# Experts of a hybrid diffusion step: four buffers for gathered rows in place of two, slot lists made in other memory, other waits for weights

## The chip, the cores and the metric

One core of a Trainium2 chip runs the whole step as one program. The metric is device time in microseconds (us) of that core; the median of three runs is compared.

## The reference

Two trunk layers work on 640 tokens (512 latent, 128 context) of width 1024 in float32. Layer 0 has HGRN2 heads beside latent attention, layer 1 gated convolution channels beside a convolution module. Each layer ends with a hierarchical mixture of experts, and only this part is touched here:

```python
p_group = softmax(t @ w_group); g_sel = argmax(p_group); p_g = max(p_group)
e_in = expert logits inside the chosen group; top_v, top_i = top_k(e_in, 2)
w_top = softmax(top_v) * p_g
hid = silu(t @ w_gate[e]) * (t @ w_up[e])      # 32 experts, FF = 128
out = sum over the two chosen e of w_top * (hid @ w_down[e])
x = layer_norm(ALPHA * x + gate * out)         # R5 holds the rows of this gate
```

## The kernel before

One program per engine, written by hand; semaphores set the order. A layer comes in this order: projections and mixer, output projection with normalisation and router, experts, combination.

*Router and lists.* VectorE works out the choice of each token and then the lists of rows of each slot (lines 1753 to 1820). A slot block has SL = 64 rows of one expert. Two blocks make a pair, so the 32 experts are NP0 = 16 main pairs (numbered 0 to 15). Experts with more than 64 rows spill into extra blocks, which are done in rounds ("quads") of two extra pairs. This data has one round in layer 0 (extra pairs 16 and 17 below) and two in layer 1 (16 to 19). HOT, PAIR, SLOT and other work areas of the lists lie in the tile mix_cm (OTF, lines 456 to 460). The lists end up in TIY, and rows_ready tells of them: first the gather rows, then the scatter rows.

*Weights.* SyncE loads three matrices of 128 x 1024 float32 words (0.52 MB) for each expert, six loads per pair (load_expert, line 643). There are four weight slots, pair u using slot u % 4; the words of slot 3 lie in scratch and in mix_cm, on top of the list areas (EXPERT_AT, line 574). So in front of pair 3 SyncE waits for rows_ready (line 710), and for pair u it waits until pair u - 4 is done (at_least(sp, m["down"], u - 3), line 711). Extra pairs use slots 0 and 1 and wait for down at 15 and 16, that is for main pairs 14 and 15, at line 723, and in the second round for the extra pair two before.

*Rows.* GpSimd gathers the rows of a pair from h_rows in memory into XG, two buffers (line 827), and scatters the results from ZT, two buffers, into expert_rows (line 833). In its loop (lines 848 to 865) it waits for the turn of pair u, issues the gather of u + 2, waits for the results of u in ZT (ya, yv), and issues the scatter of u. At pairs 6, 8 and 10 it has some other work (residual rows, two loads of normalisation rows).

*Computation of a pair.* TensorE turns the gathered rows (turn, line 2461, 8 transposes), multiplies by gate and up (gate_up, line 2473, 32 products), turns the hidden values (2480) and multiplies by down (2490, 8 products). In the order of its program: gate_up(u), turn(u + 1), turn_hidden(u), down(u). ScalarE and VectorE copy halves of the turned rows and of the results.

*R5.* The gate rows of the combination, 128 x 2048 words in scratch words 4096 to 6143, are loaded by SyncE before the output projection of their layer (lines 688 and 695) and used at line 1900. G1, the gate rows of the first residual, lies in GR; it is last used at line 1730, before the lists are made.

*Combination.* When all scatters are done (moe_done, line 889) SyncE loads expert_rows back, TensorE sums them with their weights (line 2005), and the second normalisation follows.

Of the kernel before, what the change touches and what calls it, by code (L numbers as in the profile page):

```python
# [17 lines left out]
KD = D // 128  # L18
NT = 5
NLAT = 512  # L20
NTOK = 640
# [19 lines left out]
NCOL = NPAIR + 2  # L41
# [169 lines left out]
def build(nc, A, O):  # L211
# [7 lines left out]
    with ctx:  # L219
# [101 lines left out]
        def moe_sems(l):  # L321
            names = ["w0", "w1", "w2", "w3", "wd0", "wd1", "wd2", "wd3", "xw0", "xw1", "xwd0", "xwd1", "g0", "g1", "t", "xa", "xv", "gu", "sg", "hid", "ht", "hc",
                     "down", "ya", "yv", "s0", "s1", "s_ix", "pool_passed"]
            return {n: sem(f"moe{l}_{n}") for n in names}
        MS = [moe_sems(l) for l in range(2)]


# [125 lines left out]
        XG = z(10240, 2048).rearrange("p (b d) -> p b d", b=2)  # L453
        XGT = z(12288, 2048).rearrange("p (b d) -> p b d", b=2)
        GG, GT = z(15040, 160), z(15200, 160)
        HOT = OTF[:, 512:1792].rearrange("p (i s) -> p i s", i=2 * NT)
        PAIR = OTF[:, 2100:2100 + 2 * NT * NCOL].rearrange("p (i c) -> p i c", i=2 * NT)
        SLOT, SLOTM, PNUM, INPAIR, BASE = [OTF[:, 2980 + 10 * i:2990 + 10 * i] for i in range(5)]
        ROWI, NONE = OTF[:, 3040:3040 + NCOL], OTF[:, 3080:3080 + NCOL]
        KROW = OTF[:, 3120:3120 + NCOL]  # L460
# [131 lines left out]
        def _(sp):  # L592
# [50 lines left out]
            def load_expert(l, e, p, i, first, second):  # L643
                m = MS[l]
# [8 lines left out]
                sp.dma_start(expert_gu(p, i)[:, 0:1024], g).then_inc(m[f"{first}{p}"], 16)  # L653
                sp.dma_start(expert_gu(p, i)[:, 1024:2048], u).then_inc(m[f"{first}{p}"], 16)
                sp.dma_start(expert_down(p, i), dn).then_inc(m[f"{second}{p}"], 16)

            for l in range(2):
# [29 lines left out]
                if l == 0:  # L687
                    load_rows(0, 5, R5, d_g1)
                else:
# [5 lines left out]
                    load_rows(1, 5, R5, d_g1)  # L695
# [8 lines left out]
                for u in range(NP0):  # L704
# [4 lines left out]
                    if u == 3:  # L709
                        sp.wait_ge(rows_ready, 2 * l + 2)  # L710
                    at_least(sp, m["down"], u - 3)
                    for i in range(2):
                        load_expert(l, 2 * u + i, u % 4, i, "w", "wd")
# [3 lines left out]
                with sp.If(quads > 0):  # L717
                    with sp.Fori(0, quads) as j:
                        for u in range(4):
                            e = sp.value_load(EXI[0:1, bass.ds(j * 4 + u, 1)], min_val=0, max_val=NE - 1)  # L720
                            if u % 2 == 0:

                                sp.wait_ge(m["down"], j * 2 + (NP0 - 1 + u // 2))
                            load_expert(l, e, u // 2, u % 2, "xw", "xwd")
# [14 lines left out]
        def _(pool):  # L739
# [53 lines left out]
            for l in range(2):  # L793
# [32 lines left out]
                def gather(par, rows):  # L826
                    nc.gpsimd.indirect_dma_start(  # L827
                        out=XG[:, par, :], out_offset=None, in_=HD[:, :],
# [1717 lines left out]
```

## Time and profile before

| | us |
|---|---|
| median of three runs | 1415.01 (1414.82 to 1421.27) |
| the profiled execution | 1423.75 |
| its span, first to last instruction | 1421.9 |
| TensorE busy | 1197.5 (84%) |
| VectorE busy | 574.1 (40%) |
| ScalarE busy | 344.5 (24%) |
| GpSimd busy | 188.9 (13%) |
| moved by DMA | 266.59 MB, mean 187 GB/s |
| chain that ended last: TensorE 69%, DMA 16%, VectorE 7% | |

The busy share is an average over stages with different limits. The expert stage of layer 0 lies at about 640 to 830 us, that of layer 1 at about 1175 to 1381 us. Of the chain, 10% are gathers (scratch<-h_rows), 2% loads of w_up. In the rows below, L2461 is line 2461, PE is TensorE, SPq the queue of SyncE, and a window's DMA share is the mean busy share of the 16 DMA engines.

### The profile page before, as it was taken

The numbers are of one execution on the slowest core, as the hardware profiler recorded it, in microseconds if no ns is written. First come the engines' busy times: TensorE is split into PE (matmuls) and PEld (weight loads), VectorE is DVE, ScalarE is ACT, GpSimd is POOL, SyncE is SP. The second block draws the span as 40 slices with busy tenths as digits, with TensorE's granted clock in tenths as the row PEclk, the third lists the DMA queues.
The fourth block names the chain that finished last, engine by engine and source line by source line (L and its number), as shares of the span: only waits on it lengthen the run. The fifth ranks groups of instructions, "written<-read, shape, count | busy, mean of one in ns | idle before, by whom it ended". The sixth has DMA issues, their size and how long they took to land.

```text
span 1421.9 us, 17080 instructions
## 1 busy us (share of the span) xinstructions
PE 1197.5 (84%) x6597; PEld 696.4 (49%) x6597; DVE 574.1 (40%) x1123; ACT 344.5 (24%) x687; POOL 188.9 (13%) x175
## 2 busy tenths in 40 slices
PE   4999999999999989966877767999979966877755
PEld 2554455555465764544544434555544544544432
DVE  2123332200456665552311133199946552311217
ACT  1334444311145441111111115110132111111112
POOL 1000000000000010301332115200000301242120
PEclk9999999999999999976988988999998977989987
DMA  9423566833101061075999763211102065999764
GB/s 342 164 98 132 192 229 240 311 109 139 47 19 67 9 249 60 30 274 188 409 409 388 274 245 119 94 59 60 60 0 104 30 262 201 403 410 402 260 236 176
DMA packets 98369, 266.59 MB, mean 187 GB/s; under 512 B 12572, under 2 KB 14883, under 8 KB 97139
## 3 DMA queue, kind: packets, MB, share of 16 engines
q1 hardware_dynamic: 82176, 230.36, 43.0%
q0 software_dynamic: 15792, 35.04, 6.6%
q8 instruction: 53, 0.87, 0.2%
q14 instruction: 26, 0.21, 0.0%
q10 hardware_dynamic: 322, 0.12, 0.0%
HBM read 257.65 MB, written 28.79 MB: 201 GB/s over the span
## 4 chain that ended last, share of the span: by engine, by line
PE 69%; DMA 16%; DVE 7%; issue 3%; ACT 3%; SPq 1%; ACTq 0%; POOL 0%; POOLq 0%; DVEq 0%
PE ps L2034 17%; PE ps L2045 15%; DMA scratch<-h_rows,gather_scatter_rows 10%; PE ps L2473 5%; PE ps L2490 4%; PE ps L1953 3%; PE ps L2170 3%; PE ps L2461 2%; DMA weights<-in_moe_w_up 2%; PE ps L2332 2%; PE ps L2313 2%; PE ps L2137 1%; PE ps L2005 1%; PE ps L2057 1%; PE ps L2187 1%
## 5 line engine op out<-in xcount | busy, mean ns | idle before, releaser
L2034 PE MATMUL ps<-h_cm,weights 128*128 128x512 f32 (+1 forms) x896 | 247.2, 438 | 1.1 <-ACT h_cm L961 1.1
L2034 PEld LDWEIGHTS ps<-h_cm,weights 128*128 128x128 f32 x896 | 137.0, 192 | 115.1 <-issue 114.8
L2045 PE MATMUL ps<-weights,mix_cm 128*128 128x512 f32 x288 | 127.3, 600 | 1.0 <-ACT mix_cm L1147 1.0
L2473 PE MATMUL ps<-weights,scratch 128*64 128x256 f32 x704 | 90.5, 414 | 14.9 <-DMA weights<-in_moe_w_up 13.0
L1612 DVE SCALAR_TENSOR_TENSOR scratch<-scratch,taps_cm 128x655 f32<-128x655 f32 x120 | 101.5, 897 | 2.5 <-ACT scratch L1196 1.0
L2461 PE MATMUL ps<-consts,scratch 128*128 128x128 f32 x304 | 50.3, 316 | 60.5 <-DMA scratch<-h_rows,gather_scatter_rows 60.5
L2045 PEld LDWEIGHTS ps<-weights,mix_cm 128*128 128x128 f32 x288 | 54.7, 192 | 67.0 <-issue 66.9
L2473 PEld LDWEIGHTS ps<-weights,scratch 128*64 128x64 f32 x704 | 62.8, 151 | 47.8 <-issue 34.9
L2045 PE MATMUL ps<-weights,h_cm 128*128 128x512 f32 (+1 forms) x240 | 83.3, 506 | 2.8 <-DMA weights<-in_ab_w_in 2.8
L2461 PEld LDWEIGHTS ps<-consts,scratch 128*128 128x128 f32 x304 | 41.4, 199 | 76.8 <-DMA scratch<-h_rows,gather_scatter_rows 48.2
L1857 DVE TENSOR_TENSOR scratch<-ps,scratch 128x128 f32<-128x128 f32 x38 | 11.1, 291 | 131.2 <-ACT scratch L1236 131.1
L2045 PEld LDWEIGHTS ps<-weights,h_cm 128*128 128x128 f32 x240 | 42.4, 194 | 43.5 <-issue 40.4
L833 POOL DMA_INDIRECT expert_rows<-scratch,gather_scatter_rows x32 | 33.1, 1034 | 196.6 <-ACT scratch L1242 140.8
L1544 DVE SCALAR_TENSOR_TENSOR mix_cm<-mix_cm,gate_rows,ps 128x128 f32<-128x128 f32 x152 | 46.0, 345 | 28.7 <-PE ps L2278 26.6
L1867 DVE COPY scratch<-ps 128x512 f32<-128x512 f32 x38 | 26.3, 691 | 69.9 <-PE ps L2490 69.9
L1289 DVE COPY mod_parts<-ps 128x512 f32<-128x512 f32 x24 | 16.6, 691 | 93.6 <-PE ps L1953 93.6
L2490 PE MATMUL ps<-weights,scratch 128*64 128x512 f32 x176 | 45.3, 635 | 9.6 <-issue 6.4
L1228 ACT ACTIVATE scratch<-ps 128x512 f32<-128x512 f32 x38 | 22.7, 597 | 120.2 <-PE ps L2461 120.2
L827 POOL DMA_INDIRECT scratch<-h_rows,gather_scatter_rows x36 | 37.0, 1026 | 69.8 <-DVE router_small L1820 44.6
L1242 ACT ACTIVATE scratch<-ps 128x512 f32<-128x512 f32 x38 | 22.7, 597 | 88.9 <-PE ps L2490 88.9
L819 POOL DMA_DIRECT2D h_rows<-scratch x10 | 5.7, 574 | 280.0 <-DVE scratch L1693 280.0
L1236 ACT ACTIVATE scratch<-ps 128x128 f32<-128x128 f32 x38 | 10.6, 278 | 131.7 <-PE ps L2473 131.7
(405 smaller groups left out, 1875.7 us busy)
## 6 DMA issues: line engine op xcount, KB each, us to landing
weights<-in_mod_w SPq DMA_DIRECT2D x13, 2048.0 KB, 8.8
weights<-in_moe_w_gate SPq DMA_DIRECT2D x44, 512.0 KB, 9.1
weights<-in_moe_w_up SPq DMA_DIRECT2D x44, 512.0 KB, 10.8
weights<-in_moe_w_down SPq DMA_DIRECT2D x44, 512.0 KB, 11.6
x_tm<-in_mod_w SPq DMA_DIRECT2D x10, 2048.0 KB, 8.7
weights<-in_ab_w_in SPq DMA_DIRECT2D x6, 2048.0 KB, 12.0
weights<-in_cd_w_in SPq DMA_DIRECT2D x5, 2048.0 KB, 15.9
h_cm<-in_moe_w_gate SPq DMA_DIRECT2D x16, 512.0 KB, 11.1
```

Source lines behind the costliest of these rows:

```text
L827: nc.gpsimd.indirect_dma_start(out=XG[:, par, :], out_offset=None, in_=HD[:, :], in_offset=bass.IndirectOffsetOnAxis(ap=rows, axis=0), bou ...
L833: nc.gpsimd.indirect_dma_start(out=YD[:, :], out_offset=bass.IndirectOffsetOnAxis(ap=rows, axis=0), in_=ZT[:, par, :], in_offset=None, bou ...
L1544: ins = V.scalar_tensor_tensor(out=nxt, in0=state_before(i, n, step, hh), scalar=HE[:, u % 2, at:at + 1], in1=bank(4 + j)[:, hh * 128:hh * ...
L1612: ins = V.scalar_tensor_tensor(out=CO[:, j, 0:655], in0=UP[:, j, k:k + 655], scalar=CW[:, 4 * k + j:4 * k + j + 1], in1=CO[:, j, 0:655], o ...
L1953: ins = T.matmul(ps("mod", l, c)[32 * j:32 * j + 32, 0:512], CT[:, k, :], w[:, k, :], start=(k < 4), stop=(k >= 4))
L2034: ins = T.matmul(ps(*name)[:, a:b], w[:, k, col:col + 128], HT[:, k, a:b], start=(k == 0), stop=(k == KD - 1))
L2045: ins = T.matmul(ps(*name)[:, at:at + w.shape[2]], src[:, k, t * 128:t * 128 + 128], w[:, k, :], start=(k == 0), stop=(k == KD - 1))
L2170: ins = T.matmul(ps("s", 2 * p + i, t)[:, a:b], q[rows, tc], k[rows, ka:ka + b - a], start=(rope == 0), stop=(rope == 1))
L2313: ins = T.matmul(bank(3), w[:, k, j * 128:j * 128 + 128], HT[:, k, 0:512], start=(k == 0), stop=(k == KD - 1))
L2461: ins = T.transpose(turned_bank(k // 4)[:, (k % 4) * 128:(k % 4) * 128 + 128], rows[:, k, :], ident)
L2473: ins = T.matmul(pair_bank(u)[SL * i:SL * i + SL, 0:256].rearrange("p (g f) -> p g f", g=2), XGT[:, u % 2, at:at + SL], w[:, k, :, :], sta ...
L2490: ins = T.matmul(result_bank(u, b)[SL * i:SL * i + SL, :], HIDT[:, u % 2, SL * i:SL * i + SL], w[:, b * 512:b * 512 + 512], start=True, st ...
```

## The change

- XG becomes four buffers. The two new ones lie in scratch words 4096 to 6143, the words of R5. The gather of pair u + 4 is issued at the turn of pair u; four gathers are issued at the start. Buffers 2 and 3 have semaphores of their own (gathered), shared by both layers.
- The areas of the slot lists (HOT, PAIR, SLOT and so on) move from mix_cm to GR, the tile of G1. The wait for rows_ready in front of pair 3's weights goes.
- The extra pairs' weights wait for x_slot, which GpSimd raises after the results of main pairs 12 and 13, and in the rounds after those of each extra pair.
- R5 is no longer loaded by SyncE before the output projection, but by GpSimd at pair 15, after its turn; VectorE waits for it (d_r5) where it used to wait for d_g1.
- The weights' semaphores are shared by both layers (pair_gu, pair_down), with values counted on, and TensorE's loop is written out for main and extra pairs. Its order of work is the same.

The core of the diff, without renamings that go with it:

```diff
-        XG = z(10240, 2048).rearrange("p (b d) -> p b d", b=2)
+        XG = [z(10240, 1024), z(11264, 1024), z(4096, 1024), z(5120, 1024)]
-        HOT = OTF[:, 512:1792].rearrange("p (i s) -> p i s", i=2 * NT)
-        PAIR = OTF[:, 2100:2100 + 2 * NT * NCOL].rearrange("p (i c) -> p i c", i=2 * NT)
-        SLOT, SLOTM, PNUM, INPAIR, BASE = [OTF[:, 2980 + 10 * i:2990 + 10 * i] for i in range(5)]
+        HOT = GR[:, 0:1280].rearrange("p (i s) -> p i s", i=2 * NT)
+        PAIR = GR[:, 1280:1280 + 2 * NT * NCOL].rearrange("p (i c) -> p i c", i=2 * NT)
+        SLOT, SLOTM, PNUM, INPAIR, BASE = [GR[:, 1600 + 10 * i:1610 + 10 * i] for i in range(5)]
@@ SyncE
-                if l == 0:
-                    load_rows(0, 5, R5, d_g1)
-                else:
+                if l == 1:
                     retire(LAST_IN_SLOT1[1])
...
                     load_rows(1, 3, R3, d_r)
-                    load_rows(1, 5, R5, d_g1)
...
-                    if u == 3:
-                        sp.wait_ge(rows_ready, 2 * l + 2)
                     at_least(sp, m["down"], u - 3)
                     for i in range(2):
-                        load_expert(l, 2 * u + i, u % 4, i, "w", "wd")
+                        load_expert(l, 2 * u + i, u % 4, i, pair_gu[u % 4], pair_down[u % 4])
...
-                                sp.wait_ge(m["down"], j * 2 + (NP0 - 1 + u // 2))
-                            load_expert(l, e, u // 2, u % 2, "xw", "xwd")
+                                sp.wait_ge(m["x_slot"], j * 2 + (1 + u // 2))
+                            load_expert(l, e, u // 2, u % 2, m[f"xw{u // 2}"], m[f"xwd{u // 2}"])
@@ GpSimd
-                for u in range(2):
+                for u in range(4):
                     gather(u, TIY[:, 0, u:u + 1])
...
                     pool.wait_ge(m["t"], u + 1)
-                    pool.wait_ge(m[f"g{par}"], 16 * (u // 2 + 1))
-                    gather(par, TIY[:, 0, u + 2:u + 3])
+                    pool.wait_ge(g_sems[u % 4], (64 * l if u % 4 > 1 else 0) + 16 * (u // 4 + 1))
+                    if u < NP0 - 2:
+                        gather(u % 4, TIY[:, 0, u + 4:u + 5])
+                    elif u == NP0 - 1:
+
+                        pool.wait_ge(d_mod, MOD_DMAS * 2)
+                        pool.dma_start(R5, MODD[l, 3].partition_broadcast(128)).then_inc(d_r5, 16)
 
                     pool.wait_ge(m["ya"], u + 1)
                     pool.wait_ge(m["yv"], u + 1)
+                    if u in (NP0 - 4, NP0 - 3):
+
+                        pool.sem_inc(m["x_slot"], 1)
                     at_least(pool, m[f"s{par}"], 16 * (u // 2))
                     scatter(par, TIY[:, 1, u:u + 1])
...
                             pool.wait_ge(m["ya"], j * 2 + (NP0 + u + 1))
                             pool.wait_ge(m["yv"], j * 2 + (NP0 + u + 1))
+                            pool.sem_inc(m["x_slot"], 1)
@@ VectorE
-                dve.wait_ge(d_g1, 32 if l == 0 else 48)
+                dve.wait_ge(d_g1, 16 * (l + 1))
...
-                dve.wait_ge(d_g1, 32 * (l + 1))
+                dve.wait_ge(d_r5, 16 * (l + 1))
@@ TensorE
-                    pe.wait_ge(m[f"g{u % 2}"], g0 + 16 * (u // 2 + 1))
+                    pe.wait_ge(landed, value)
```

## Rows read from the trace of the kernel before

**Rows 1.** Who TensorE waits for, 640 to 835 us: us in total, times, longest.
```profile
PE ps L2461 <- DMA scratch<-h_rows,gather_scatter_rows: 30.5, 8, 9.5
...
PE ps L2473 <- DMA weights<-in_moe_w_up: 5.1, 2, 4.4
```

**Rows 2.** Stretches: us; PE, PEld, DVE, ACT, POOL busy; clock, DMA share, GB/s.
```profile
660.00:664.00 4.00, 4.00 (x29) 2.62 (x26) 0.29 (x1) 0.28 (x1) 0.00 (x0) 0.78 0.02 5
667.00:784.00 117.00, 90.97 (x620) 57.70 (x616) 28.65 (x72) 18.47 (x38) 37.52 (x32) 0.90 1.01 394
680.00:700.00 20.00, 17.73 (x133) 11.52 (x133) 9.11 (x27) 4.14 (x8) 5.32 (x5) 1.00 1.03 408
784.00:803.00 19.00, 16.81 (x107) 9.85 (x107) 4.03 (x9) 2.94 (x6) 4.01 (x4) 0.91 0.52 177
1200.00:1317.00 117.00, 90.92 (x631) 57.87 (x627) 28.75 (x72) 18.64 (x39) 37.52 (x32) 0.91 1.00 395
1317.00:1333.00 16.00, 14.04 (x98) 8.41 (x98) 4.03 (x9) 2.85 (x6) 4.01 (x4) 1.00 0.57 188
```

**Rows 3.** Timeline of TensorE: start us, us, line, shapes, [idle before <- releaser].
```profile
657.56 5.72 PE L2473 MATMUL ps<-weights,scratch 128*64 128x256 f32 x32 [0.88 <-DVE scratch L1849]
...
663.21 1.16 PE L2461 MATMUL ps<-consts,scratch 128*128 128x128 f32 x8
...
670.28 1.16 PE L2461 MATMUL ps<-consts,scratch 128*128 128x128 f32 x8
...
719.85 1.97 PE L2461 MATMUL ps<-consts,scratch 128*128 128x128 f32 x8 [3.25 <-DMA scratch<-h_rows,gather_scatter_rows]
...
784.21 1.71 PE L2461 MATMUL ps<-consts,scratch 128*128 128x128 f32 x8 [2.68 <-DMA scratch<-h_rows,gather_scatter_rows]
...
808.53 5.33 PE L2473 MATMUL ps<-weights,scratch 128*64 128x256 f32 x32 [4.37 <-DMA weights<-in_moe_w_up]
...
818.18 3.67 PE L2473 MATMUL ps<-weights,scratch 128*64 128x256 f32 x32 [0.75 <-DMA weights<-in_moe_w_up]
...
823.30 1.94 PE L2490 MATMUL ps<-weights,scratch 128*64 128x512 f32 x8 [0.43 <-DVE scratch L1861]
...
1360.19 5.36 PE L2473 MATMUL ps<-weights,scratch 128*64 128x256 f32 x32 [3.51 <-DMA weights<-in_moe_w_up]
...
1369.24 3.67 PE L2473 MATMUL ps<-weights,scratch 128*64 128x256 f32 x32
```

**Rows 4.** Timeline of SyncE: issues of expert weights, start us and us.
```profile
646.34 0.33 SPq L653 DMA_DIRECT2D scratch<-in_moe_w_gate  x1
...
666.93 0.33 SPq L653 DMA_DIRECT2D weights<-in_moe_w_gate  x1
...
796.41 0.36 SPq L653 DMA_DIRECT2D weights<-in_moe_w_gate  x1
...
1348.92 0.35 SPq L653 DMA_DIRECT2D weights<-in_moe_w_gate  x1
```

**Rows 5.** Chain that ended last: start us, us, what.
```profile
646.99 7.62 DMA scratch<-h_rows,gather_scatter_rows
...
767.33 3.68 PE ps L2490 x8
...
1068.98 16.84 PE ps L2057 x32
```

**Rows 6.** The gather, line 827: time to landing of all 42.
```profile
DMA to landing us min/median/max: 2.1/8.1/13.2
```

**Rows 7.** Timeline of VectorE at the output projection of layer 1.
```profile
1079.72 2.29 DVE L1720 TENSOR_TENSOR scratch<-scratch,ln_rows 128x2048 f32<-128x2048 f32 x1 [8.68 <-DMA scratch<-mod_rows]
...
1086.58 1.22 DVE L1730 TENSOR_TENSOR scratch<-ps,gate_rows 128x1024 f32<-128x1024 f32 x1
```

**Rows 8.** What the DMA engines moved from 664 to 818 us.
```profile
DMA packets 16998, 55.13 MB, mean 358 GB/s; under 512 B 3566, under 2 KB 3566, under 8 KB 16987
...
q1 hardware_dynamic: 12091, 44.03, 73.4%
```

## What the change is expected to do

> **What bounds the kernel now.** I read four views in this order: who TensorE waits for in the expert stage of layer 0, the stretches of both expert stages, what the DMA engines carried, and then the single instructions.
>
> The first view says that TensorE waits 30.5 us in 8 long pieces for gathered rows and only 5.1 us for expert weights, both of these in the extra pairs [rows 1]. Taken alone, this asks for more gather buffers. The second view corrects it. From the first release of a weight slot to about the landing of the last main weights, 667 to 784 us, the DMA engines are busy at 1.01 and carry 394 GB/s, and in layer 1 they do the same from 1200 to 1317 us [rows 2]. So in those 117 us the gather is late because it shares engines that are already full. Twelve pairs of weights come in there, 117 / 12 = 9.75 us per pair. TensorE alone needs 7.07 us per pair at full clock (two successive turns, 663.21 and 670.28) [rows 3]. The bound is DMA bandwidth, and the gather wait is where it shows.
>
> Behind this stretch the engines fall to 0.52 for 19 us (177 GB/s); in layer 1 it is 0.57 for 16 us [rows 2]. The reason is in the issues: the first extra weights leave at 796.41 us, when pair 14 is done [rows 4], though their slot was last used by pair 12. TensorE meanwhile works off pairs 13 to 15 with nothing coming in behind them. There is another hole before the first release: the engines are at 0.02 from 660 to 664 us [rows 2], since all four slots are full.
>
> **The change part by part.** I count in bytes and in the time at which the last extra weights can be used, because everything behind that (last pair, scatter, reading back, combining) is untouched.
>
> *Slot lists in other memory, no wait before the fourth pair.* Today the weights of pair 3 leave at 646.34 us [rows 4], beside the first gather, which takes 7.62 us on the chain [rows 5]; gathers go down to 2.1 us and have a median of 8.1 us [rows 6]. Pair 3 will leave right behind pair 2, near 632 us, and its 3.15 MB (two experts, three matrices of 0.52 MB) take 8 us at 394 GB/s; queued behind pairs 0 to 2 they are in by about 648 us. The first gather should then land at 5 to 6 us, so the first release comes at about 664.5 instead of 666.93 us [rows 4]: 2.4 us earlier (bounds 0 and 3.5). In layer 1 the loads start later against the router, and I take 1.5 us. The vector instructions that make the lists are the same ones; only their addresses differ, and I cost that at nothing.
>
> *Four gather buffers.* A gather for pair u+4 is issued at the turn of pair u, so each has some 28 us for what takes 8.1 us, at most 13.2 us [rows 6]. The 30.5 us wait goes. What is late next is the weights: TensorE catches up with them after some eight pairs and then waits 9.4 - 7.07 = about 2.3 us in each pair. This part alone gives little at the rate of the stream. It gives TensorE's position: at the end of the stream it is at most one pair behind the weights, where today it has three or four pairs to do. It also moves two gathers, 0.6 MB, into the empty stretch before the first release.
>
> *Extra weights after pairs 12 and 13 (x_slot).* Today their release waits for pairs 14 and 15. Now they follow pair 15's weights with hardly a pause, so the hole at 784 to 803 us closes. x_slot is raised by GpSimd, in line with its gathers and scatters; behind the results of pair 12 this is some 1 us later than TensorE's own signal, while two to three pairs of weights are queued at the DMA engines. The second round in layer 1 has only these two slots and keeps its dependence on the first extra pair; there I charge the 1 us.
>
> *R5 moved to the end of the main pairs.* 128 x 2048 x 4 bytes = 1.05 MB go into the full stream: +2.6 us at 408 GB/s, hidden behind nothing in layer 0, since the last weights are behind it. The load is on GpSimd's queue, ahead of the scatter of pair 15 and of the extra pairs; the scatter's buffer is wanted two pairs, some 18 us, later, and R5 itself only in the combination. Its removal from the beginning of a layer frees nothing on the path: in layer 1 VectorE does wait 8.68 us for such rows [rows 7], but the first result of the output projection is ready at 1085.82 us [rows 5] and VectorE, through with its row operations, takes it up at 1086.58 [rows 7]; I take 0 (bounds 0 and 1 us). The added wait on d_mod there has been satisfied for long.
>
> *Sum for layer 0.* From 664 to 818 us 55.13 MB were moved, 44.03 MB of them on the queue of the weights, which is 14 pairs [rows 8]. Of the new order the same stretch holds + 1.05 (R5) - 0.6 (two gathers), about 55.6 MB. At 394 GB/s that is 141 us, at 408 GB/s (the rate inside the full stretch, 680 to 700 us, without its ramp at the start [rows 2]) 136 us. With the release at 664.5 the last extra weights are in at 800.8 to 805.6 us; I take 803. Today the last extra pair's products begin at 818.18 us [rows 3]. Gain 15 us (bounds 12.5 and 17.5).
>
> *Sum for layer 1.* The first two extra pairs come 15 us earlier as well: weights at about 1327 and 1336 us. The first of them ends at 1334, its slot is refilled from 1335, and from issue to use that took 1360.19 - 1348.92 = 11.3 us [rows 3, 4]: 1346.3. The last pair's slot is free at 1343.4 + 1; with the same 11.3 us its products begin at 1355.7 us, against 1369.24 now [rows 3]: gain 13.5 us (bounds 9 and 17).
>
> *Clock.* After a wait TensorE may begin at its low level: 4.37 us of idle cost the 32 products 5.33 instead of 3.67 us, 3.25 us gave a turn of 1.97 us, 2.68 us one of 1.71 instead of 1.16 us [rows 3]. My 2.3 us waits lie just below these. I charge 0.75 us for the last pair of each layer, 1.5 us.
>
> Total 15 + 13.5 - 1.5 = 27 us. The span 1421.9 becomes 1394.9, and the profiled execution's time of 1423.75 becomes 1396.8. The three runs of the kernel before had 1415.01 as their median, 8.7 us under that execution. Subtracting the same 27 us gives 1388.
>
> One rule of the Trainium skill speaks against this: "DMA: Bandwidth & Descriptors", section Specifications, gives about 358 GB/s as what memory yields to one core. By it 55.6 MB would need 155 us and layer 0 would gain nothing (819.8 against 818.18). The trace disagrees: 394 GB/s stand for 117 us in both layers [rows 2].
>
> **The rivals.**
> *The early loads work, the deeper gathers don't help.* GpSimd works in order, so each gather still stands behind the results and the scatter before it; if gathers slow as the weight queue deepens, TensorE keeps today's pace and only the hole is filled. Extra weights are then in before TensorE gets to them: 4 us of waiting and 1.7 us of low clock in front of the first extra pair [rows 3] and about 1 us before the second go, 6.7 us per layer, some 14 in all: 1401. Against: at the worst seen, 13.2 us [rows 6], a gather four pairs ahead is still in time. Chance 0.15.
> *More than forecast.* The stream holds 408 GB/s, no wait costs clock, the second round of layer 1 is as dense as the first: 17.5 + 17, 1380. Chance 0.12.
> *It doesn't do what it says.* A second wait of the same length (the shared semaphores, a GpSimd order that holds x_slot back until pair 15, or the memory rate of the page) leaves the last extra weights where they are: 1411 to 1419. Chance 0.07.
> *Slower, through the clock.* Every pair now has a wait for weights. If it suffices to drop the clock each time, a pair costs 7.07 + 0.81 (turn 1.97 for 1.16) + 2.05 (products 5.72 for 3.67) + 1.74 (second products 3.68 for 1.94) = 11.7 us [rows 3, 5]. Fourteen pairs from 686 us then end at 850, where today the end is 825.2 [rows 3]; with layer 1 that is +50 us, 1465. It decides from a mean pair of (825.2 - 686) / 14 = 9.94 us, that is when over 62% of the pairs run low. Against it: a pair at the low level outlasts the 9.4 us in which weights arrive, so its wait vanishes and TensorE, busy without a break, gets its clock back, as within the products of 657.56 [rows 3]. The skill has it too ("TensorE: Matmul & The Clock Gate", section HAM oscillation): a wait for DMA in every tile can throttle each tile anew; the stretch 667 to 784, with its longer waits, ran at 0.90 [rows 2]. Chance 0.04.
>
> **How the numbers follow.** The forecast has the remaining 0.62; its own range is 1382 to 1397 (gains of 33 and 18 us, near the bounds of the two sums). The range of 8 in 10 takes in the better case, with up to 3 us more should both starts gain their full 3.5 us, and just the partial one: 1377 to 1402. A measurement of this kernel can tell 0.5%, 7 us, from no change. Faster by more, under 1408: 0.62 + 0.15 + 0.12 = 0.89. Within 0.5%: 0.07. Slower by more: 0.04.
>
> **What would show it.** Right: TensorE's wait for gathered rows nearly gone and in its place some ten waits of 2 to 3 us for weights per layer; the DMA engines at 1.0 from about 665 to 800 us without the hole; first extra weights issued near 776 us instead of 796.41; the fourth pair's near 632; the last extra pair's products at about 803 and 1355 us; R5 landed before the combination. Wrong: a hole that stays, gathers over 20 us, a mean pair of 9.75 us although the gathers are in, the low clock in most pairs, or a combination that waits for R5.

## The result and the profile after

The changed kernel takes 1404.85 us (median of 10 runs, 1401.88 to 1408.92). The kernel before, run in the same sessions, takes 1420.51 us (median of 10, 1407.82 to 1424.74). The ratio is 0.990 with a 95% interval of 0.988 to 0.993: the kernel became 1.0% faster, about 14 us. The prediction had the direction right, forecast 27 us and 1388 us, and its range ended at 1402. Of the 16.9 us by which 1388 was missed, 5.5 us are the starting point (the three runs I counted from had a median of 1415.0, ten have 1420.5); the larger part is the gain itself.

| | before | after |
|---|---|---|
| profiled execution, span | 1421.9 us | 1402.6 us |
| expert stage, layer 0 | 178.25 us | 172.65 us |
| expert stage, layer 1 | 195.21 us | 186.62 us |
| weights of pair 3 issued | 646.34 us | 625.62 us |
| first weight slot free, after the first gather's issue | 19.9 us | 16.8 us |
| first extra weights issued | 796.41 us | 771.60 us |
| last extra pair's products begin, layer 0 | 818.18 us | 804.40 us |
| last extra pair's products begin, layer 1 | 1369.24 us | 1348.88 us |

"Expert stage" is from the issue of the first gather to the end of the last extra pair's second products. I use it because the two profiled executions do not start it at the same time: the first gather of layer 0 leaves at 646.99 us before [rows 5] and at 641.78 us after. Those 5.2 us are not the change's: of two experiments below, e5, which is the kernel before with one constant altered, issues it at 642.49 us in its profile, and e4, which has the change, at 647.76 us. At least in part they come from stretches in which the older execution had a low clock (the same 32 records of products near 535 us took 15.57 us there and 13.97 us here). The spans differ by 19.3 us: 5.2 so, 5.6 in the stage of layer 0, 8.6 in that of layer 1, and nothing left over. The stages give 14.2 us, as does the ratio of the runs (1.0%); the two medians lie 15.7 us apart.

Who TensorE waits for after the change, 630 to 830 us (us in total, times, longest); the rows answer to [rows 1]:

```profile
PE ps L2014 <- DMA scratch<-expert_rows: 10.3, 1, 10.3
PE ps L2482 <- DMA weights<-in_moe_w_up: 7.6, 3, 3.4
PE ps L2470 <- DMA scratch<-h_rows,gather_scatter_rows: 6.3, 1, 6.3
PE ps L2482 <- DMA h_cm<-in_moe_w_up: 6.3, 2, 3.5
...
PE ps L2482 <- DMA mix_cm<-in_moe_w_up: 5.7, 2, 3.2
```

Of the 30.5 us in 8 waits for gathered rows one wait is left, that for the first gather, with nothing of the stage ahead of it to hide behind: 6.3 us, 9.5 before. The 21 us of the others are gone. In their place stand 7 waits for expert weights, 19.6 us in all, where the kernel before had 2 with 5.1 us. `weights`, `h_cm` and `mix_cm` are the memories of different slots, so these three rows are one cause. That is the picture the prediction drew. The first row is the read-back behind the stage, which nobody touched.

The next view is what explains the miss: stretches of the kernel after (us; PE, PEld, DVE, ACT, POOL busy; granted clock, DMA share, GB/s), answering to [rows 2].

```profile
658.00:784.00 126.00, 103.52 (x688) 61.18 (x686) 31.51 (x78) 20.61 (x42) 38.45 (x33) 0.92 1.01 397
784.00:792.00 8.00, 6.88 (x49) 4.02 (x46) 1.71 (x4) 1.31 (x3) 1.57 (x2) 1.00 1.03 414
792.00:796.00 4.00, 2.83 (x27) 1.97 (x26) 0.95 (x2) 0.76 (x2) 1.83 (x3) 1.00 0.86 350
796.00:800.00 4.00, 3.57 (x28) 2.19 (x26) 1.18 (x3) 0.88 (x2) 0.39 (x1) 1.00 0.41 161
800.00:804.00 4.00, 1.03 (x6) 0.15 (x2) 0.69 (x1) 0.60 (x1) 0.86 (x2) 0.95 0.24 96
804.00:808.00 4.00, 3.60 (x18) 2.37 (x20) 0.00 (x0) 0.00 (x0) 1.57 (x3) 0.50 0.13 41
```

The engines are full from 658 to 792 us without the hole of 0.52 that [rows 2] had behind 784 us. But they do not stop together. The share falls over 12 us, 0.86, 0.41, 0.24, 0.13: a few engines are still at work while most have nothing to do. And TensorE waits for just those. The chain that ended last has this in it (start us, us, what):

```profile
641.78 4.45 DMA scratch<-h_rows,gather_scatter_rows
...
783.35 20.82 DMA weights<-in_moe_w_up
...
804.40 6.65 PE ps L2482 x32
```

This load, the second w_up of the last extra pair and the fifth of its six loads, takes 20.82 us from its issue, and the products start only when its last piece is in. TensorE's timeline shows that the wait then costs a second time:

```profile
775.75 5.36 PE L2482 MATMUL ps<-h_cm,scratch 128*64 128x256 f32 x32 [2.77 <-DMA h_cm<-in_moe_w_up]
...
793.79 3.67 PE L2482 MATMUL ps<-weights,scratch 128*64 128x256 f32 x32 [1.17 <-DVE scratch L1858]
...
804.40 6.64 PE L2482 MATMUL ps<-weights,scratch 128*64 128x256 f32 x32 [3.37 <-DMA weights<-in_moe_w_up]
...
812.49 1.94 PE L2499 MATMUL ps<-weights,scratch 128*64 128x512 f32 x8 [0.43 <-DVE scratch L1870]
...
1340.05 5.07 PE L2482 MATMUL ps<-weights,scratch 128*64 128x256 f32 x32 [3.58 <-DMA weights<-in_moe_w_up]
...
1348.88 3.67 PE L2482 MATMUL ps<-weights,scratch 128*64 128x256 f32 x32 [0.20 <-DMA weights<-in_moe_w_up]
```

The "32 products" of this document are 32 records: the code has 16 gate and up products for a pair (8 steps for each of two experts), and the trace records each twice. The 32 records take 3.67 us at 2.4 GHz. Behind waits of 2.77, 3.37 and 3.58 us they take 5.36, 6.64 and 5.07 us, at the low level (1.2 GHz) for more than half of it; the stretch 804 to 808 us has a granted clock of 0.50.

### The profile page after: what moved, and what is told of

Read it like the earlier page. It is cut to its first block, busy times and chain, and to the rows that moved or that the text cites. A ratio compares the mean times of both kernels' runs of the same rounds, so it can differ in the third digit from the quotient of the medians.

```text
span 1402.6 us, 17080 instructions
## 1 busy us (share of the span) xinstructions
PE 1194.3 (85%) x6597; PEld 685.8 (49%) x6597; DVE 574.2 (41%) x1123; ACT 344.5 (25%) x687; POOL 190.0 (14%) x177
## 4 chain that ended last, share of the span: by engine, by line
PE 65%; SPq 13%; DMA 8%; DVE 7%; ACT 3%; issue 3%; ACTq 0%; POOLq 0%; DVEq 0%; POOL 0%
PE ps L2043 18%; PE ps L2054 15%; PE ps L2482 4%; SPq L658 4%; SPq L656 4%; SPq L657 4%; DMA weights<-in_moe_w_up 3%; PE ps L1962 3%; PE ps L2179 3%; PE ps L2341 2%; PE ps L2499 2%; PE ps L2322 1%; PE ps L2146 1%; PE ps L2014 1%; PE ps L2470 1%
## 5 line engine op out<-in xcount | busy, mean ns | idle before, releaser
L2482 PE MATMUL ps<-weights,scratch 128*64 128x256 f32 x704 | 96.2, 434 | 26.3 <-DMA weights<-in_moe_w_up 23.3
L2470 PE MATMUL ps<-consts,scratch 128*128 128x128 f32 x304 | 45.7, 295 | 13.2 <-DMA scratch<-h_rows,gather_scatter_rows 13.2
L1245 ACT ACTIVATE scratch<-ps 128x128 f32<-128x128 f32 x38 | 10.6, 278 | 181.7 <-PE ps L2482 181.7
L2470 PEld LDWEIGHTS ps<-consts,scratch 128*128 128x128 f32 x304 | 38.1, 195 | 28.5 <-issue 28.5
L2482 PE MATMUL ps<-scratch 128*64 128x256 f32 x128 | 35.4, 440 | 8.9 <-DMA mix_cm<-in_moe_w_up 8.9
L2482 PE MATMUL ps<-h_cm,scratch 128*64 128x256 f32 x256 | 34.4, 428 | 8.9 <-DMA h_cm<-in_moe_w_up 8.8
```

What stands on the lines that cost most here:

```text
L2470: ins = T.transpose(turned_bank(k // 4)[:, (k % 4) * 128:(k % 4) * 128 + 128], rows[:, k, :], ident)
L2482: ins = T.matmul(pair_bank(u)[SL * i:SL * i + SL, 0:256].rearrange("p (g f) -> p g f", g=2), XGT[:, u % 2, at:at + SL], w[:, k, :, :], sta ...
```

## The experiments

**Theory and rivals.** The mean share had done what the byte count said: from the full stretch to the tail, nothing was missing. So the theory (A) was: the rows of gathers and scatters are spread unevenly over the 16 engines. Each expert has 64 places in a pair's 128, and its tokens fill them from the first partition upward; places without a token are skipped. If an engine serves fixed partitions, those with low ones carry more rows on top of an equal share of the weights, and the last load lands when the fullest engine is through. The rivals were that the deeper gathers or the early extra weights did not do what they should, that R5's 1.05 MB were the burden, and that the deeper queue itself lets the engines drift apart.

All medians stand beside that of the kernel before on the same chip, and "under it" is the distance between the two; "stages" is the sum of the two expert stages in the one profiled execution (before 373.5, after 359.3), good to some us.

| kernel | median us (n) | before | under it | ratio, 95% | stages |
|---|---|---|---|---|---|
| the changed kernel | 1404.85 (10) | 1420.51 | 15.7 | 0.988 to 0.993 | 359.3 |
| e1_spread | 1395.47 (6) | 1417.55 | 22.1 | 0.982 to 0.989 | 348.0 |
| e2_gather_two_ahead | 1413.44 (10) | 1417.55 | 4.1 | 0.994 to 0.998 | 361.0 |
| e3_extras_late | 1408.00 (9) | 1417.55 | 9.5 | 0.992 to 0.996 | 364.0 |
| e4_r5_behind | 1402.24 (4) | 1417.55 | 15.3 | 0.984 to 0.993 | 351.2 |
| e5_before_spread | 1413.59 (10) | 1418.13 | 4.5 | 0.995 to 1.001 | 364.1 |
| e6_spread_r5 | 1393.55 (6) | 1418.13 | 24.6 | 0.981 to 0.987 | 343.7 |
| e7_eights | 1413.06 (10) | 1418.13 | 5.1 | 0.996 to 1.001 | 363.8 |
| e8_spread_r5_order | 1389.59 (6) | 1418.13 | 28.5 | 0.978 to 0.985 | 341.6 |
| e9_order_and_busy | 1389.10 (6) | 1418.97 | 29.9 | 0.974 to 0.982 | 339.2 |
| e10_three_pairs | 1418.05 (10) | 1418.97 | 0.9 | 0.996 to 1.001 | 368.4 |

The changed kernel was not run again beside these ten, and the kernel before stood 1.5 to 3 us higher in its sessions than in theirs. So a difference to 1404.85 us has that much in doubt beside the noise; where it matters, both the distance of the medians and that of the column "under it" are given.

**e1_spread: the same tokens in other partitions.** Only a constant changes, the place that each rank of an expert gets. Eight successive ranks now fall into eight different groups of four partitions.

```diff
-    put("iota_h", slice(None), p[None, :] - (SL - 0.5))
+    r = np.arange(SL)
+    place = 8 * (r % 8) + (r // 8 + 4 * (r % 8 >= 4)) % 8
+    rank = np.argsort(place)
+    put("iota_h", slice(None), (SL * (p // SL) + rank[p % SL])[None, :] - (SL - 0.5))
```

> The changed kernel with one constant altered: the 64 places of a block are taken in an order that goes round the partition groups, so that the about 40 rows which a block holds on average lie evenly over all groups of partitions, in place of the first 40. Nothing is left out. In the changed kernel the last extra weights of layer 0 land at 804 us although the mean DMA share falls to 0.43 at 796 us: a few of the 16 engines are behind. Theory A (the rows of gathers and scatters lie unevenly, and the engines that serve the first places get up to twice the rows): the tail with few engines vanishes, the last extra weights are used 5 to 8 us earlier after the first gather in each layer, 1393 us (1388 to 1397). Theory B (the engines drift apart for another reason, such as unequal speed or the depth of the queue): the tail stays, within 3 us of the changed kernel's 1405.

Measured: 1395.47 us, 9.4 us under the changed kernel (6.4 us by the distances to the kernel before), with the same 17080 instructions and, to 0.01 MB, the same bytes. The tail of the stream of e1 in layer 0 (stretches, columns as above) and, from TensorE's timeline, the last pair's products:

```profile
792.00:796.00 4.00, 4.00 (x30) 2.34 (x26) 0.00 (x0) 0.00 (x0) 0.00 (x0) 0.74 1.02 404
796.00:800.00 4.00, 3.36 (x20) 1.61 (x17) 1.26 (x4) 0.96 (x3) 0.00 (x0) 1.00 0.58 234
800.00:804.00 4.00, 3.67 (x32) 2.65 (x32) 0.61 (x1) 0.54 (x2) 1.39 (x3) 1.00 0.09 32
```

```profile
800.26 3.67 PE L2485 MATMUL ps<-weights,scratch 128*64 128x256 f32 x32 [0.47 <-DMA weights<-in_moe_w_up]
```

The share stays at 1.02 until 796 us and is at 0.09 from 800 us on, where it was 0.24 and 0.13 before the edit. The engines end together. The last pair's wait shrinks from 3.37 to 0.47 us, its products run in 3.67 us. The stages are 165.03 and 183.01 us; the prediction's own sums, 15 - 0.75 and 13.5 - 0.75 us off the stages before, were 164.0 and 182.5. So the sum was right, to about 1 us, for engines that share evenly, and theory A has its mechanism. Its size was smaller than expected: against the first gather the last pair's products begin 4.7 us earlier than in the changed kernel in layer 0 (157.97 for 162.62) and 3.6 us in layer 1, not 5 to 8; the other 3.0 us are the clock of the last pair in layer 0, which I had not counted. Nor is it the tail alone: the first extra weights leave 124.4 us after the first gather, 129.8 in the changed kernel, which fits late engines that hold up the pairs inside the full stretch too.

**e7_eights: which partitions belong together.** The same idea with another step: successive ranks eight partitions apart and nothing else.

```diff
-    rank = np.argsort(8 * (r % 8) + (r // 8 + 4 * (r % 8 >= 4)) % 8)
+    rank = np.argsort(8 * (r % 8) + r // 8)
```

> As e1, but rank r of a block goes to place 8 * (r % 8) + r / 8: for each run of eight neighbouring partitions the same number of rows, but only the first four partitions of each eight are taken up to rank 31. If an engine serves eight neighbouring partitions, this is as even as e1: 1395. If it serves groups of four partitions that alternate (partitions 4n to 4n + 3), then every second group gets up to twice the rows and the time is that of the changed kernel, 1405, or up to 5 us more.

Measured: 1413.06 us, 8.2 us slower than the changed kernel (10.6 by the distances) and so somewhat beyond what I expected. Against e6, run beside it, it is 19.5 us slower, of which e6's other edit, R5 moved, may account for 2 to 3 us. The stretches of e7:

```profile
792.00:796.00 4.00, 2.98 (x16) 1.46 (x16) 1.38 (x2) 1.20 (x2) 0.57 (x1) 1.00 1.00 413
796.00:800.00 4.00, 1.57 (x8) 1.02 (x10) 0.00 (x0) 0.00 (x0) 1.66 (x3) 0.76 0.69 274
800.00:804.00 4.00, 4.00 (x30) 2.38 (x28) 0.06 (x1) 0.28 (x1) 0.00 (x0) 0.82 0.51 201
804.00:808.00 4.00, 3.17 (x20) 1.52 (x20) 1.81 (x4) 1.20 (x2) 0.00 (x0) 1.00 0.36 146
```

Here about half the engines are still busy (0.51) where in e1 almost none is. In this order the first 32 ranks of an expert lie in partitions whose number divided by eight leaves 0 to 3: every other group of four. That they load half the engines, while e1's order loads all, says that partitions 0 to 3 of each eight and partitions 4 to 7 are served by different engines. Four neighbouring partitions as the unit fit this; a smaller unit was not ruled out by a run. The Trainium skill has this ("DMA: Bandwidth & Descriptors", section The descriptor swizzle), for full transfers to 128 partitions: an engine writes four partitions and the four that lie 32 further on, engines 0 to 7 the lower half and 8 to 15 the upper. By that rule e7 puts an expert's first 32 rows on four of its eight engines, and e1 spreads each eight rows over all eight; 1413 and 1395 us agree with it, for gathers and scatters that skip rows too. The trace names no engine by number, so which one is late is not shown. In the stages e7 lies 4.5 us above the changed kernel, less than in the medians.

**e5_before_spread: e1's edit on the kernel before.**

> The kernel before with the one altered constant of e1 (rows of a block spread evenly over the partition groups). Theory A (uneven rows make a few DMA engines late) holds for this kernel as well, but here TensorE works off three pairs behind the last main weights, and a late engine is hidden there; gathers may land a little earlier in the full stretch. Expected 1414 (1409 to 1418) beside a kernel before at 1417. If the even rows are worth the same 10 us here as on the changed kernel, the unevenness limited the full stretch itself, not only what is last to land.

Measured: 1413.59 against 1418.13 us, ratio 0.998 with an interval of 0.995 to 1.001: no more than 7 us and not to be told from nothing. The stage sum is 9.4 us shorter in its one profile, more than the medians bear out. I had expected the unevenness to cost little in the kernel before, because a late engine there has three pairs of work and a hole of 19 us to catch up in. The medians allow that and don't show it: up to 7 us in the interval stand beside 6 to 9 us for the same edit on the changed kernel. The trace speaks against a full cover. Against the first gather, e5 issues its first extra weights 6.0 us earlier than the kernel before (143.4 for 149.4), and this gain arises ahead of the hole. That the change made the unevenness dearer is therefore argued and not shown; shown is that even rows are worth having in the changed kernel.

**e2_gather_two_ahead: two gathers in flight, everything else as changed.**

```diff
-                for u in range(4):
+                for u in range(2):
                     gather(u, TIY[:, 0, u:u + 1])
...
-                    if u < NP0 - 2:
-                        gather(u % 4, TIY[:, 0, u + 4:u + 5])
-                    elif u == NP0 - 1:
+                    gather((u + 2) % 4, TIY[:, 0, u + 2:u + 3])
+                    if u == NP0 - 1:
```

> The changed kernel, but only two gathers are issued at the start and the gather of pair u + 2 is issued at the turn of pair u, as before the change; extra weights, lists and R5 stay as changed. If the deeper gathers carry the gain, TensorE waits some 30 us for gathered rows in each layer again and the time goes back by 7 us or more, to 1412 or above, since only the hole behind the main weights is filled. If the early extra weights carry it (the rival of the prediction), it stays at 1405 within 3 us.

Measured: 1413.44 us, 8.6 us slower than with four (11.6 by the distances). Waits of TensorE in e2, whole span:

```profile
PE ps L2469 <- DMA scratch<-h_rows,gather_scatter_rows: 53.6, 16, 7.0
```

The waits for gathered rows are back, 16 of them in the two layers. So the deeper gathers carry more than half of the whole gain, and the rival of 1401 us ("the deeper gathers don't help") falls by its mechanism, though its number came nearest. The profiled execution of e2 is the fastest of its ten, 5 us below the median; its stage sum is not to be set against the medians.

**e3_extras_late: the first extra weights wait for pairs 14 and 15 again.**

```diff
-                                sp.wait_ge(m["x_slot"], j * 2 + (1 + u // 2))
+                                sp.wait_ge(m["down"], j * 2 + (NP0 - 1 + u // 2))
```

> The changed kernel, but the extra pairs' weights wait for main pairs 14 and 15 again in place of x_slot; four gather buffers stay. Theory: a pair of extra weights needs about 11 us from issue to use; with the wait back, the hole of about 15 us in the DMA engines comes back, and the time is 1412 to 1420. If the deeper gathers alone carried the gain it would stay at 1405 within 3 us.

Measured: 1408.00 us, only 3.2 us slower than the changed kernel (6.1 by the distances); I had expected 1412 to 1420. Stretches of e3 and, from SyncE's timeline, its first issue of extra weights:

```profile
776.00:780.00 4.00, 4.00 (x36) 2.60 (x37) 0.02 (x1) 0.28 (x1) 0.91 (x1) 1.00 0.55 217
780.00:784.00 4.00, 2.76 (x16) 1.15 (x14) 1.85 (x4) 1.19 (x2) 0.00 (x0) 1.00 0.24 96
```

```profile
783.37 0.36 SPq L656 DMA_DIRECT2D weights<-in_moe_w_gate  x1
```

The hole is back, from 776 to 784 us, with the first extra weights at 783.37 instead of 771.60 us. It is short because TensorE, with four gathers ahead, is close behind the weights and frees the slots soon. And in it the late engines can catch up, so part of what the hole costs is what the unevenness would have cost anyway. That second half is a reading of the two shares, not shown by a run. The parts add up to 8.6 + 3.2 = 11.8 us by the medians and to 17.7 us by the distances, of 15.7 us for the whole change. So they carry most or all of it, and what is left for the earlier start can't be told. In the one profile all of e3's loss lies in layer 1 (191.9 for 186.6 us); its stage of layer 0 is as long as the changed kernel's (172.1 for 172.7).

**e4_r5_behind: R5 behind the extra weights, on SyncE's queue.**

```diff
-                        pool.wait_ge(d_mod, MOD_DMAS * 2)
-                        pool.dma_start(R5, MODD[l, 3].partition_broadcast(128)).then_inc(d_r5, 16)
...
+                sp.wait_ge(m["t"], NP0)
+                sp.dma_start(R5, MODD[l, 3].partition_broadcast(128)).then_inc(d_r5, 16)
```

> The changed kernel, but R5 is loaded by SyncE behind the extra weights in place of GpSimd ahead of them. Its 1.05 MB leave the full stretch in layer 0. By the byte count of the prediction this gives 2.6 us in layer 0 and little in layer 1: 1402 us. If the last weights hang on a few late engines, R5, which is spread evenly, still costs each engine its share and the gain is the same 2 to 3 us; if it was hidden, 0. The combination doesn't wait for it in either case (it begins some 25 us later).

Measured: 1402.24 us, 2.6 us under the changed kernel's median, which is what 1.05 MB at 408 GB/s come to. With four runs the two ranges overlap, and by the distances to the kernel before the gain is nothing (15.3 for 15.7 us), so no gain of e4 by itself is shown. Its one profile has stages 8.1 us shorter than those of the changed kernel, more than the medians bear out. In the trace SyncE issues it at 793.26 us, right behind the last extra weights, outside what the last pair waits for:

```profile
790.74 2.30 SPq L658 DMA_DIRECT2D weights<-in_moe_w_down  x1
793.26 0.90 SPq L725 DMA_DIRECT2D scratch<-mod_rows  x1
```

**e6_spread_r5: e1 and e4 together.**

> The changed kernel with e1's even rows and e4's R5 behind the extra weights together. If both take their share of the same last landing, they add: e1 was 10 us below the changed kernel, e4 2 to 3 us, together 1392 (1389 to 1395). If R5 only mattered because an engine was late, it adds nothing to e1's 1395.

Measured: 1393.55 us, another 1.9 us off e1 (2.5 by the distances). It lies within the range for adding, but the ranges of the two kernels' runs overlap; that R5 costs its 2 to 3 us in the full stretch is likely by e4 and e6 together and not settled.

**e10_three_pairs: a shallower queue of weights.** The rival to theory A that was left: with four pairs in flight the engines drift apart, whatever the rows do. Here the weights of pair u wait for pair u - 2.

```diff
-                    at_least(sp, m["down"], u - 3)
+                    at_least(sp, m["down"], u - 2)
```

> The changed kernel, but the weights of a main pair wait for the pair three before in place of four before (one slot stands empty), so fewer loads are queued at the DMA engines. Rows lie as in the changed kernel. Rival theory: the depth of the queue is what lets engines drift apart, and with less of it the tail at the end shortens and the time falls under 1402. Theory A (the uneven rows): a shallower queue takes no row from the late engines; the quick ones run dry earlier, the mean DMA share falls under 1.0 and the time is 1405 to 1412.

Measured: 1418.05 us, 13 us slower than the changed kernel, and slower than either theory said. Stretches of e10 and, from SyncE's timeline, the issue of pair 3's weights:

```profile
658.00:796.00 138.00, 107.28 (x725) 60.76 (x721) 32.64 (x81) 21.21 (x44) 40.01 (x35) 0.94 1.02 400
...
800.00:804.00 4.00, 3.28 (x16) 1.97 (x18) 0.00 (x0) 0.00 (x0) 1.05 (x1) 0.50 0.78 310
```

```profile
657.73 0.33 SPq L656 DMA_DIRECT2D scratch<-in_moe_w_gate  x1
```

The share stays at 1.02, so three pairs in flight fill the engines as well as four; theory A's sentence that it would fall under 1.0 was wrong too. And the tail is still there with the shallower queue: 0.78 from 800 to 804 us, then 0.36 and 0.13. What is lost is the start: pair 3's 3.15 MB leave at 657.73 us instead of 625.62 and join the full stretch, where they cost their 8 us. The rival, by which fewer pairs in flight should have shortened the tail, falls by the shares; the time alone could not say so, since the edit also delays pair 3. That the late fourth pair is the whole of the 13 us was not tested by itself; the stages of the profile are 9.1 us longer.

**e8_spread_r5_order and e9_order_and_busy: the versions that beat both.** e8 loads the gate and up weights of both experts of a pair first, then both down weights, since the first products need only the former. e9 adds 12 products in front of the first extra pair of each round, to keep TensorE busy through its wait; they write columns of the pair's bank that nothing reads.

```diff
+                    for what in ("gu",), ("down",):
+                        for i in range(2):
+                            load_expert(..., what)
...
+                    if u == 0:
+                        for _ in range(12):
+                            T.matmul(pair_bank(u)[:, 384:512], const("ones")[:, 0:128], const("tri"), start=True, stop=True)
```

> e6 and, in addition, for each pair the four gate and up loads are issued ahead of the two down loads, in place of expert by expert. Where TensorE waits for weights, the products of gate and up can begin one load of 0.52 MB earlier (1.3 us), and the down weights have the 3.7 us of these products to land in. On the path this counts once in layer 0 and for the extra pairs in layer 1: 2 to 3 us under e6, 1389. If the waits are set by an engine that is late with everything, the order changes nothing.

> e8 with 12 products of 128 x 128 into unused columns of the pair's bank, done by TensorE before it waits for the weights of the first extra pair of each round; their results are not used. They take 2 to 3 us of a wait of 2.8 to 3.6 us. Theory: a wait of over about 2.7 us costs the 32 products behind it 1.5 to 3 us, because they begin at the low clock; with the wait filled they take 3.7 us. In layer 1 this is on the path once or twice: 1387 to 1388 beside 1389.6 for e8. If the wait has become shorter than the filling, the time rises by up to 1 us per round.

Measured: e8 1389.59 us, 4.0 us under e6, which ran beside it, and 15 us under the changed kernel (12.9 by the distances). Of the two places where I expected the gain, the profile shows one: the stage of layer 0 is as long as e6's (162.4 for 162.6 us), that of layer 1 2.0 us shorter. e9 1389.10 us. In TensorE's timeline of layer 1 the first extra pair's products do what the filling was for. e8:

```profile
1323.58 5.36 PE L2486 MATMUL ps<-weights,scratch 128*64 128x256 f32 x32 [3.08 <-DMA weights<-in_moe_w_up]
```

e9, the filling in layer 0 (each product of this type is recorded twice) and then the products of layer 1:

```profile
789.17 2.84 PE L2541 MATMUL ps<-consts 128*128 128x128 f32 x24
...
1324.47 3.67 PE L2486 MATMUL ps<-weights,scratch 128*64 128x256 f32 x32 [0.26 <-issue]
...
1333.36 3.67 PE L2486 MATMUL ps<-weights,scratch 128*64 128x256 f32 x32 [1.64 <-DMA weights<-in_moe_w_up]
```

5.36 becomes 3.67 us, but the medians differ by 0.5 us and the distances by 1.4, less than they can tell, and 1387 to 1388 was expected. The filled pair is not the last: the one behind it now waits 1.64 us for its weights, where in e8 it did not wait. Against the first gather its products begin 1.1 us earlier than in e8 (170.99 for 172.05), so about a third of the 1.7 us saved is given back there.

## Why the prediction was right or wrong

**What bounds the kernel: right.** DMA bandwidth in the full stretch, 394 GB/s before, 397 after; the gather wait was where it showed. When it went, waits for weights took its place, 7 in layer 0 and 11 in layer 1 where I said some ten, in layer 0 of 1.8 to 3.5 us where I said 2 to 3. (The 9.4 us of weights per pair in the prediction stand without their working; they are its 9.75 us at 408 in place of 394 GB/s.)

**The steps with a time.** On the clock of the kernel before (5.2 us added) the fourth pair's weights leave at 630.8 us (predicted near 632) and the first extra weights at 776.8 (predicted near 776). R5 is issued at 787.35 us, lands 10.1 us later, and VectorE first uses it in the combination at 831.63 us: landed before, as said. The first release moved forward by 3.1 us against the first gather (2.4 predicted, bounds 0 and 3.5); that gather landed in 4.45 us where I said 5 to 6.

**The step that failed: "With the release at 664.5 the last extra weights are in at 800.8 to 805.6 us".** It divides bytes by the mean rate of 16 engines and takes the result for the time at which the last load can be used. The first half was right. Behind 792 us the shares of the windows add up to (0.86 + 0.41 + 0.24 + 0.13) x 4 = 6.6 us of work for all engines; shared evenly, it would have ended at 798.6 us, 140 us after the first release at 658.6, where the prediction had 138.5 us. But the last pair's products began at 804.40, 5.8 us later, when the latest engine was through. Taken against the first gather, the last weights can be used 8.6 us earlier than before (171.19 before, 162.62 after) where I had 15, below even the lower bound of 12.5. The bounds were for the mean rate, and none was for the spread of the engines. In layer 1 it is 8.6 us where 13.5 were forecast, just under its lower bound of 9. e1 shows the cause by taking most of it away: with even rows alone the last weights of layer 0 can be used 13.2 us earlier than before (12.2 in layer 1), within the bounds of both sums, and the stages come out within about 1 us of the forecast.

**The clock: mis-sized.** I charged 0.75 us per layer, since my waits of 2.3 us lay just below those that had cost something. The wait before the last pair was 3.37 us and its products 6.64 instead of 3.67: 3.0 us in layer 0. Of its gain of 8.6 us, 5.6 are left. In layer 1 the last pair was warm, and all 8.6 stay. This follows from the first error: the wait got longer than foreseen because the last engine was late.

**The rivals.** "Slower, through the clock" did not come; the stretch 658 to 784 us ran at a granted clock of 0.92, where 667 to 784 had 0.90 before. "It doesn't do what it says" falls by the issue times. The result lies nearest to "the early loads work, the deeper gathers don't help", but e2 and e3 show the parts the other way round: 8.6 us for the gathers, 3.2 us for the early extra weights (11.6 and 6.1 by the distances). That its number came near is chance. I had credited the closing of the hole to the early extra weights. But TensorE's nearness to the weights closes over a third of it by itself: what the engines leave unused is (1 - 0.52) x 19 = 9.1 us in the kernel before [rows 2] and, with the windows beside the two shown (0.91 from 772 us, 0.87 from 784 us), (0.09 + 0.45 + 0.76 + 0.13) x 4 = 5.7 us in e3.

**The memory rate.** The prediction put the trace's 394 GB/s against the 358 GB/s that the Trainium skill gives ("DMA: Bandwidth & Descriptors", section Specifications). The trace was right to be believed: 397 GB/s over 126 us after the change, 400 GB/s over 138 us in e10.

**The range.** The profiled execution fell by 19.3 us, 5.2 of them the accident of where the older one's clock was low; the medians of ten fell by 15.7. A range from 1377 to 1402 missed 1404.85 by 2.85 us. Counted from the 1420.5 us of ten runs instead of 1415.0 it would have been 1382.5 to 1407.5 and have held the result; that would have been luck, since the gain was 14 to 16 us and not 27 either way. The range held the mean-rate bounds of the sum and one partial case, and no case in which the loads move as planned and still land late.

## What to carry to other kernels

When nothing but a DMA stream is left on the path, the time at which the last load can be used is that of the fullest engine. Put a tail on the mean: look at how the share falls at the end of a full stretch (1.02, 0.58, 0.09 is even; 0.86, 0.41, 0.24, 0.13 is not), and ask which small transfers beside the big ones lie on few partitions. Rows gathered for a list that is filled from the front and left open behind are such transfers; giving list places to partitions in another order changes no instruction and was worth 6 to 9 us here, beside the 14 of the whole change. Price a part of a change by what is left when it alone is undone, since two parts that fill the same hole can't both be credited with it.

## What was not expected of the hardware

- Gathers and scatters that skip rows load the DMA engines by the partitions that the rows lie in: the same rows in three orders over the partitions gave 1395.5 (e1), 1404.9 (as changed) and 1413.1 us (e7).
- SyncE's issues grow long while the DMA engines are full. Else 0.33 to 1 us long, they take up to 5.01 us in the full stretch of layer 0:

```profile
687.94 0.44 SPq L657 DMA_DIRECT2D weights<-in_moe_w_up  x1
688.43 4.57 SPq L658 DMA_DIRECT2D weights<-in_moe_w_down  x1
...
701.89 5.01 SPq L657 DMA_DIRECT2D weights<-in_moe_w_up  x1
```

  and the chain of the changed kernel puts 13% of the span on it:

```profile
PE 65%; SPq 13%; DMA 8%; DVE 7%; ACT 3%; issue 3%; ACTq 0%; POOLq 0%; DVEq 0%; POOL 0%
```

  The DMA share from 658 to 784 us is 1.01, so I read this as a sign of the bound and not as a cost of its own; no run tests it.
- Waits of 2.8 to 3.6 us put the 32 products behind them at 5.1 to 6.6 us instead of 3.67, and how much it is does not follow from the wait alone (3.58 us gave 5.07, 3.37 us gave 6.64). The prediction put waits of 2.3 us just below those that cost something; in these runs they lie on both sides (2.27 us gave 5.36 in e4, 2.26 us gave 3.67 in e3).
